# Hybrid decoder step on one core: the last down weight's low parts move from GpSimd to VectorE, and the closing tiles move forward

## The reference, cut to what matters

```python
h = h + jnp.concatenate([y_conv, y_ret], axis=-1) @ w_out
hn2 = rmsnorm(h, norm_mlp)
h = h + jnp.square(jax.nn.relu(hn2 @ w_up)) @ w_down      # w_down: 4096 x 1024, f32
y_prompt = rmsnorm(hp, norm_final)[:, N_META:]
y_sample = rmsnorm(hs, norm_final)
```

## Time and profile before

| | |
|---|---|
| median of 3 runs | 1129.34 us (1129.16 to 1129.98) |
| profiled execution | 1129.29 us, span 1127.4 us, mean granted TensorE clock 0.998 |
| PE busy | 1116.3 us, 99% of the span |
| DVE, POOL, ACT busy | 785.9, 560.2, 418.8 us |
| HBM traffic | 133 GB/s over the span |

### The profile page before, as it was taken

How to read it: one execution, slowest core, us unless ns; L and a number is a source line. 1 busy time by engine, 2 the same in 40 slices (tenths; PEclk the granted TensorE clock), 3 DMA queues, 4 the chain that set the end, 5 groups by cost and what they waited for, 6 DMA issues and landing times.

```text
span 1127.4 us, 21934 instructions
## 1 busy us (share of the span) xinstructions
PE 1116.3 (99%) x8351; PEld 1097.5 (97%) x8351; DVE 785.9 (70%) x1170; ACT 418.8 (37%) x864; POOL 560.2 (50%) x542
## 2 busy tenths in 40 slices
PE   9999999999999999999999999999999999999997
PEld 7799999999999999999999999999999999999996
DVE  5555656566466766888776777767877777877856
ACT  6422313123124343543333333335552544444424
POOL 0054253252240601142322323224999899999995
PEclk9999999999999999999999999999999999999999
DMA  8951341422323232155344353438962444464314
GB/s 221 236 138 52 97 120 49 130 75 77 94 77 96 77 113 76 60 186 188 114 151 151 133 177 114 151 114 299 328 192 75 153 151 149 134 189 151 94 38 151
DMA packets 188347, 151.41 MB, mean 134 GB/s; under 512 B 33086, under 2 KB 150566, under 8 KB 188256
## 3 DMA queue, kind: packets, MB, share of 16 engines
q1 hardware_dynamic: 183159, 146.98, 41.6%
q10 hardware_dynamic: 5096, 3.20, 0.9%
HBM read 105.44 MB, written 44.73 MB: 133 GB/s over the span
## 4 chain that ended last, share of the span: by engine, by line
PE 97%; issue 1%; DMA 1%; SPq 0%; POOL 0%; POOLq 0%; DVE 0%
PE pair L2127 19%; PE pair L2128 19%; PE pair L2129 19%; PE pair L1921 8%; PE pair L1923 8%; PE pair L1922 8%; PE pair L2106 3%; PE pair L2105 3%; PE pair L2104 3%; PE pair L1979 1%; PE pair L1980 1%; PE pair L1982 1%; PE pair L2029 1%; PE pair L2032 1%; PE pair L2039 1%
## 5 line engine op out<-in xcount | busy, mean ns | idle before, releaser
L2127 PE MATMUL pair<-m_hi,dn_hi 128*128 128x258 f32 (+2 forms) x896 | 254.7, 284 | 0.6 <-issue 0.5
L2128 PE MATMUL pair<-b_lo,up_hi 128*128 128x258 f32 x896 | 253.6, 283 | 0.0
L2127 PE MATMUL pair<-b_hi,up_hi 128*128 128x258 f32 x896 | 253.6, 283 | 0.0
L2128 PE MATMUL pair<-m_lo,dn_hi 128*128 128x258 f32 (+2 forms) x896 | 253.6, 283 | 0.0
L2129 PE MATMUL pair<-m_hi,dn_lo 128*128 128x258 f32 (+2 forms) x896 | 253.4, 283 | 0.0
L2129 PE MATMUL pair<-b_hi,up_lo 128*128 128x258 f32 x896 | 252.2, 282 | 0.0
L1921 PE MATMUL pair<-x_hi,w_both 128*128 128x344 f32 (+2 forms) x576 | 188.6, 328 | 0.1
L1923 PE MATMUL pair<-x_hi,w_both 128*128 128x344 f32 (+2 forms) x576 | 184.5, 320 | 0.0
L1922 PE MATMUL pair<-x_lo,w_both 128*128 128x344 f32 (+2 forms) x576 | 184.2, 320 | 0.0
L1888 DVE TENSOR_TENSOR hid<-pair,hid 128x516 f32<-128x516 f32 (+2 forms) x194 | 124.6, 643 | 73.8 <-PE pair L2129 71.0
L2127 PEld LDWEIGHTS pair<-b_hi,up_hi 128*128 128x128 f32 x896 | 169.3, 189 | 1.0 <-issue 0.8
(11 more groups left out here) (232 smaller groups left out, 2052.7 us busy)
## 6 DMA issues: line engine op xcount, KB each, us to landing
m_raw<-m_dram SPq DMA_DIRECT2D x56, 516.0 KB, 4.9
m_dram<-hid SPq DMA_DIRECT2D x64, 258.0 KB, 3.7
up_raw<-w_up_dram SPq DMA_DIRECT2D x32, 512.0 KB, 4.9
dn_raw<-w_down_dram SPq DMA_DIRECT2D x128, 128.0 KB, 2.4
w_raw<-w_in_dram SPq DMA_DIRECT2D x27, 512.0 KB, 3.7
m_dram<-hid SPq DMA_DIRECT2D x16, 774.0 KB, 3.8
h_dram<-hid SPq DMA_DIRECT2D x8, 516.0 KB, 3.1
h_in<-h_dram SPq DMA_DIRECT2D x16, 258.0 KB, 6.1
```

The source lines that it names most:

```text
L2127: m_.matmul(to, shs[k], mhs[k], start=STARTS[i] and k == 0, stop=False, skip_group_check=more)
L2128: m_.matmul(to, shs[k], mls[k], start=False, stop=False, skip_group_check=more)
```

## The change

- GpSimd makes no low parts of the last weight (`wi` = 31). VectorE makes them (`last_low`), one each after the reads named in `LOW_AT`, in units 29 and 30. GpSimd goes from the last `down_sum` to its closing work, and closes unit 31 read by read, as it does units 32 to 34.
- The transposes of tiles 0 to 4 and their scalings are placed earlier (`FINAL_AT`, `NORM_AT`): from the second product of unit 32 to the last of unit 33.
- VectorE adds three of the late squares into `sq_sum` after its last read, so that `token_sums` is one product for each tile where it was three or two. ScalarE does all four `last_square` before `late_std`, and the squares of unit 33 (`piece_squares(2)`) after tile 4.
- The store of tile 6 is cut from 120 rows into 112 and 8.
- At the start ScalarE writes the first head's high part before the small transfers of the row norms; at the end of the up projection it writes the last two high parts of the first down weight before two hidden splits.

```diff
-FINAL_AT = {(NW, 6): 0, (NW + 1, 1): 1, (NW + 1, 4): 2, (NW + 1, 6): 3, (NW + 2, 2): 4}
-NORM_AT = {(NW + 1, 1): (0, 0), (NW + 1, 2): (0, 1), (NW + 1, 3): (1, 0), (NW + 1, 4): (1, 1), (NW + 1, 6): (2, 0), (NW + 2, 0): (2, 1),
-           (NW + 2, 2): (3, 0), (NW + 2, 3): (3, 1), (NW + 2, 5): (4, None)}
+FINAL_AT = {(NW, 1): 0, (NW, 3): 1, (NW + 1, 0): 2, (NW + 1, 3): 3, (NW + 1, 6): 4}
+NORM_AT = {(NW, 4): (0, 0), (NW, 5): (0, 1), (NW, 6): (1, 0), (NW + 1, 0): (1, 1), (NW + 1, 3): (2, 0), (NW + 1, 4): (2, 1),
+           (NW + 1, 6): (3, 0), (NW + 2, 0): (3, 1), (NW + 2, 2): (4, None)}
+LOW_AT = {(HALVES, 0): 0, (HALVES, 2): 1, (HALVES, 4): 2, (HALVES, 6): 3, (HALVES + 1, 1): 4, (HALVES + 1, 3): 5, (HALVES + 1, 5): 6}
...
-                    sp.dma_start(io["y_prompt"][0, r0:r0 + n - more, :], y[0:n - more, :]).then_inc(y_stored[i % 4], 16)
+                    full = n - 2 * more
+                    sp.dma_start(io["y_prompt"][0, r0:r0 + full, :], y[0:full, :]).then_inc(y_stored[i % 4], 16)
                     if more:
+                        sp.dma_start(io["y_prompt"][0, r0 + full:r0 + n - more, :], y[full:n - more, :]).then_inc(y_stored[i % 4], 16)
...
             for wi in range(NW):
                 down_sum(wi)
-                for i in range(7):
-                    down_low(wi, i)
+                if wi < NW - 1:
+                    for i in range(7):
+                        down_low(wi, i)
...
-                    pool.wait_ge(dn_read, 7 * q + (seen if q >= NW else 7))
+                    pool.wait_ge(dn_read, 7 * q + (seen if q >= NW - 1 else 7))
...
+            act.wait_ge(w_gained, 1)
+            high(0, 0, None)
             act.wait_ge(rstdx_done, XT)
...
-            act.wait_ge(w_gained, 1)
-            high(0, 0, None)
             act.wait_ge(rx_moved, 48)
...
+                        if i == 5:
+                            down_split(0, 5)
+                            down_split(0, 6)
                         for j in ((), (0,), (1,), (2,), (3,), (4, 5), ())[i]:
                             mid_split(j)
-                        down_split(0, i)
+                        if i < 5:
+                            down_split(0, i)
...
-                if i == REST:
-                    piece_squares(2)
...
-            for i in range(3):
+            piece_squares(2)
+            for i in range(4):
                 last_square(i)
             late_std(0)
-            last_square(3)
             late_std(1)
...
+            def last_low(i):
+                n = dn_slot(NW - 1)
+                dve.wait_ge(dn_ready, 7 * (NW - 1))
+                dve.wait_ge(dn_high, 7 * (NW - 1) + i + 1)
+                d.tensor_tensor(dn_lo[n][i][:, :, :], dn_source(NW - 1, i), dn_hi[n][i][:, :, :], ALU.subtract).then_inc(dn_ready, 1)
...
-                        if q >= NW and i >= 5:
+                        if q >= NW - 1 and i >= 5:
                             dve.wait_ge(closed, 3 * (q - NW + 4) + i - 4)
...
+                    if (q, p) in LOW_AT:
+                        last_low(LOW_AT[(q, p)])
...
+            for i in range(1, 4):
+                which = LAST_ORDER[i]
+                total = sq_sum[:, which % 2, :]
+                dve.wait_ge(hsq_done, GROUPS + 7 + i)
+                dve.wait_ge(ssq_done, GROUPS - 2 + 6)
+                if i > 1:
+                    dve.wait_ge(late_added, i - 1)
+                d.tensor_tensor(total, total, sq_last[:, which, :], ALU.add).then_inc(late_added, 1)
...
-                pe.wait_ge(ssq_done, GROUPS - 2 + (6 if LATE_L[j] == 0 else 5))
-                pe.wait_ge(hsq_done, GROUPS + GROUP_AT[j])
+                pe.wait_ge(late_added, LATE_ADDED[j])
+                if j:
+                    pe.wait_ge(fstd_done, FIRST_LATE + 1)
...
-                    src = [sq_sum[:, LATE_L[j], c0:c1]] + [sq_last[:, which, c0:c1] for which in GROUP[j]]
-                    for k, sq in enumerate(src):
-                        ins = m_.matmul(SUM_B[:, 2 * j + tile:2 * j + tile + 1], sq, ones[:, 0:1], start=k == 0, stop=k == len(src) - 1)
+                    ins = m_.matmul(SUM_B[:, 2 * j + tile:2 * j + tile + 1], sq_sum[:, LATE_L[j], c0:c1], ones[:, 0:1], start=True, stop=True)
...
+                if i == 0:
+                    pe.wait_ge(dn_read, 7 * NW)
```

More of the change, by code:

```diff
@@ L150 @@
 LAST_ORDER, LAST_READ = (0, 3, 1, 2), (4, 5, 6, 7)
-GROUP, GROUP_AT = ((3, 1), (2,)), (9, 10)
+LATE_ADDED = (2, 3)
 LW = EDGE[2] - EDGE[1]
@@ L357, in late_rows, with dn_source @@
             return [(acc(n, first + a)[:, EDGE[1]:EDGE[2]].unsqueeze(1), slice(a, a + 1)) for a in range(2)]
+        def dn_source(wi, i):
+            return dn_raw[wi % 2][:, 2 * A_OP[i][0] + A_OP[i][1], :, :] if i in (0, 2, 5) else dn_s[A_OP[i]][:, :, :]
         def acc(n, which):
@@ L404, in program @@
         o_done, o_read, Sinc_done, S_ready = sem("o_done"), sem("o_read"), sem("Sinc_done"), sem("S_ready")
-        std_ready, o_normed, yT_done, y_ready = sem("std_ready"), sem("o_normed"), sem("yT_done"), sem("y_ready")
+        std_ready, o_normed, y_ready = sem("std_ready"), sem("o_normed"), sem("y_ready")
         ksmp_ready, state_dec, state_new = sem("ksmp_ready"), sem("state_dec"), sem("state_new")
@@ L430, in program @@
             "fT_done", "fsq_done", "fstd_done", "frstd_done", "f_ready"))
-        d_half = sem("d_half")
+        d_half, late_added = sem("d_half"), sem("late_added")
         dve_own, passed = sem("dve_own"), sem("passed")
@@ L747, in _ @@
                     more = SAMPLES if l and c1 == HALF else 0
-                    sp.dma_start(io["y_prompt"][0, r0:r0 + n - more, :], y[0:n - more, :]).then_inc(y_stored[i % 4], 16)
+                    full = n - 2 * more
+                    sp.dma_start(io["y_prompt"][0, r0:r0 + full, :], y[0:full, :]).then_inc(y_stored[i % 4], 16)
                     if more:
+                        sp.dma_start(io["y_prompt"][0, r0 + full:r0 + n - more, :], y[full:n - more, :]).then_inc(y_stored[i % 4], 16)
                         sp.dma_start(io["y_sample"].rearrange("b s d -> (b s) d"), y[n - more:n, :]).then_inc(y_stored[i % 4], 16)
-            for i, count in enumerate((5, 3, 3, 2)):
+            for i, count in enumerate((5, 3, 4, 2)):
                 sp.wait_ge(y_stored[i], 16 * count)
@@ L882, in down_low @@
                 n = dn_slot(wi)
-                src = dn_raw[wi % 2][:, 2 * A_OP[i][0] + A_OP[i][1], :, :] if i in (0, 2, 5) else dn_s[A_OP[i]][:, :, :]
+                src = dn_source(wi, i)
                 pool.wait_ge(dn_high, 7 * wi + i + 1)
@@ L1287, in piece_squares @@
                 act.wait_ge(closed, 3 if n == 0 else 12 + 3 * n)
+                if n == 0:
+                    act.wait_ge(dn_ready, 7 * NW)
                 act.wait_ge(dn_read, 7 * (NW - 3 if n == 0 else NW + n))
```

## The result

| kernel | median us (runs) | ratio to before, 95% interval |
|---|---|---|
| before | 1129.4 (8) | |
| after | 1132.3 (8) | 1.0025, 1.0016 to 1.0034 |

The change makes the kernel 2.8 us slower (1.8 to 3.8 us by the interval). The profiled execution of after took 1131.3 us, 1.0 under its own median; its span is 1129.5, 2.1 over that of before. So the pair of traces shows 2.0 of the 2.8 us; the other 0.8 is in no trace. VectorE's reads now stand at line 1907, its low parts at 1848, its late adds at 1930; GpSimd's closing adds at 909; TensorE's products at 2156 to 2158, its transposes at 2228, the token sums at 2200.

A forecast was written before the change was run, and what follows sets the result against it. TensorE, busy for 99% of the span, was taken to bound the kernel. The terms −0.2 − 0.3 + 0.8 + 1.3 + 0.4 + 0.5 + 0 = +2.5 on 1129.29 gave 1131.8 us, range 1128.4 to 1133.4.

The forecast's parts named there:

- Start: At the kernel's start, ScalarE's high part moved ahead lets TensorE begin earlier: −0.2 us, bounds 0 to −0.4.
- First down weight: First down unit: earlier high parts shift GpSimd's phase against VectorE's hidden low part: −0.3 us, bounds −0.6 and +0.2.
- Inputs: Unit 29: VectorE's low part 1 waits for ScalarE's high part, delaying the fifth read and TensorE's seventh product: +0.8 us.
- Collision: Units 29 and 30: VectorE's low parts wait through whole GpSimd closing adds: +1.3 us, bounds 0 and +1.9.
- Closing tiles: Unit 33: uncovered wait before the seventh product, tile 2's transposes before tile 0 is scaled: +0.4 us, bounds 0 and +0.6.
- Tail: After the last product: late `add_last` and VectorE adds delay token sums, dropped passes give some back: +0.5 us.
- Stores: Store of tile 6 at the end: extra issue is covered, bytes are the same: 0 us.
- only the high part's wait counts: Rival: VectorE and GpSimd collide little, so the collision term and half the tiles' go: 1130.3 us, chance 0.25.
- the change is not slower: Rival: GpSimd reaches the last weight's sums earlier, second sum done by 1080.7, low parts cost nothing: 1128.4 us, chance 0.15.
- growing lag: Rival: low part 0 delays GpSimd's sums, low parts 2 to 5 each meet a full long add: 1133.4 us, chance 0.10.

The follow-up runs named there:

- tiles alone: Kernel before with only the closing tiles' places and the square order that belongs to them changed: 1135.34 us, ratio 1.0052.
- sums alone: Kernel before with only the late squares added by VectorE and the token sums in one pass: 1129.12 us, ratio 0.9997.
- low parts later: Kernel before with low parts on VectorE behind later reads, GpSimd's closing adds held until all are written, unit 31 closed read by read: 1132.49 us.
- free: Kernel before with late low parts on VectorE and held closing adds, unit 31 closed as before: 1129.38 us, ratio 0.9999.
- sums split: Kernel before with the first token sums' passes over sq_sum issued ahead of the wait for the last squares: 1128.6 us, ratio 0.9994.
- low parts held: Kernel before with low parts on VectorE, unit 31 closed read by read, GpSimd's closing adds waiting until all low parts are written: 1135.61 us.
- old store: The changed kernel with the 120-row store of tile 6 again: 1132.24 us, ratio 1.0026.
- transposes first: The changed kernel with the transposes of tile 5's rest and of tile 6 ahead of the token sums: 1131.73 us, ratio 1.0021.
- low parts alone: Kernel before with only the low parts moved to VectorE and GpSimd closing unit 31 read by read: 1131.67 us, ratio 1.0018.
- Split sums with the store: Kernel before with split token sums, the 112-row store and the first high part moved ahead: 1128.03 us, ratio 0.9987.

## Why the prediction was right, point by point

The prediction was 1131.8 us, the median is 1132.3. The profiled pair differs by 2.0 us where the sum gave 2.5. That the number lies so near the median is in part luck: the tail's +0.5 did not come, and the medians differ by 0.8 more than the pair, for which no trace has a place. What held is the mechanism of the two largest terms, inputs and collision, which the experiments isolate.

- **Start**, −0.2: from the eight matmuls to the first head product it is 1.84 us where the earlier trace rows have 2.10, −0.26. Right, and 1.84 too in the two kernels that have this edit without the low parts and tiles. Timeline of after:

```profile
54.12 1.06 ACT L952 ACTIVATE w_both<-w_raw 128x1024 fp32r<-128x1024 f32 x1 [1.63 <-POOL w_raw L774]
...
58.02 2.00 PE L1986 MATMUL pair<-wv_lo,x_end 128*24 128x512 f32 x8
...
59.86 0.33 PE L1950 MATMUL pair<-x_hi,w_both 128*128 128x360 f32 x1
```

- **First down weight**, −0.3: not shown. In after TensorE waits 0.37 and 0.30 us there in place of 0.54, and unit 29 comes 0.42 earlier in all. But with the same edits alone the waits summed to 1.9 us and the time did not move. How VectorE and GpSimd meet differs between executions by more than this term: among six kernels with the same code up to there (before, tiles alone, sums alone, low parts later and free, sums split), unit 29's seventh product starts between 1081.68 and 1083.49.
- **Inputs**, +0.8: 1.05. The mechanism is right: low parts held apart from GpSimd leave this loss whole, later places remove it. The size is 0.25 low, mostly because low part 0 holds GpSimd up: its first sum took 0.91 us beside it, 0.17 more than the 0.74 of a sum that meets no low part, and the second sum, on which the high part waits, moves by as much. I had this in the upper bound only.
- **Collision**, +1.3: 0.27 + 0.74 = 1.01. Shown by the held kernel: low part 2 takes 0.42 in place of 1.54 and unit 30's losses go. One by one, GpSimd's adds end at 1084.34, 1085.79, 1087.22 and 1088.82, and low parts 2 to 5, each begun inside one of them, end 0.28 to 0.29 us behind these: VectorE stood through the whole instruction each time, as the prediction had it. The size is 0.3 high because unit 29 had already lost 0.25 more; the two terms together are 2.06 where the sum had 2.1. That their sum fits so well is luck in part: GpSimd's adds began 0.37 us later against unit 29 than assumed, and a low part ended 0.28 behind an add, not the 0.55 of the earlier trace rows. The Trainium skill's exclusive lock (SBUF — State Buffer, "SBUF: two separate sides") agrees with this trace: 1.54 us for a low part that began 0.04 us into a closing add of 1.29. The Trainium skill's other rule (GPSIMD Engine Reference, "Engine selection") is about right on the price, 0.42 against GpSimd's 0.74. That price is worth nothing here, since GpSimd's low parts were not what TensorE waited for.
- **Closing tiles**, +0.4: from unit 31's seventh product to E 21.65 us (1094.76 to 1116.41) against 21.11 (1093.03 to 1114.14), +0.54. Two more traces of the changed kernel, with the old store and with the transposes first, have 21.64 and 21.62; low parts alone has 21.11. Of the 0.54, 0.34 stand at tile 2's transposes, which wait for VectorE's scaling as predicted:

```profile
1103.46 1.06 PE L2228 MATMUL pair<-ident,hid 128*128 128x128 f32 x8 [0.18 <-DVE y_out L1838]
```

- **Tail**, +0.5: −0.17. The steps up to the first scaling are right: `add_last` at E + 1.31 (predicted 1.35), first token sums E + 2.45 (2.2), first scaling +0.89 (+0.6). The difference is that VectorE's adds start 0.56 apart, not 0.4, and that the first waits for a square of ScalarE's too, done 0.07 behind `add_last`. The step that failed is the last one, from VectorE's scalings and ScalarE's half tile to the end: the last issue came 1.75 later instead of 0.2 to 0.3, and the end did not move. Half of the 1.75 is a clock of 0.50 in the transposes, which kernels with before's own tail show as well, so that half is not the change's. The sum took it that the end follows VectorE and ScalarE; the table of the tails shows slack there, and an end of −0.17 is well within its spread.
- **Stores**, 0: no difference in time with the old store.

Of the rivals, that only the high part's wait counts falls with the 1.01 us of collision; that the change is not slower falls with GpSimd's second sum, done at 1081.45 where 1080.7 was needed. The growing lag did not come: low part 0 did delay the sums, but by 0.17 us, and low parts 3 to 6 took 0.41 to 1.00 us.

What the prediction did not see: closing unit 31 read by read adds a wait of VectorE for GpSimd, and only GpSimd's lead in the changed order keeps it free.

## What to carry to other kernels

Before work moves from an idle-looking engine to the one that feeds the bottleneck, look at what stands behind it in that engine's order and when its inputs are ready: the same seven instructions cost 2.0 us in the changed places, and nothing where their inputs were there, GpSimd was held still and unit 31 was closed as before. Parts of a schedule change are not additive, so test each alone and price the waits that one part keeps free for another. At the end of a kernel, measure from the last issue to the end first; where stores fill that time, an engine finishing later or earlier may not show. And look at several traces of the same code before reading a difference of a microsecond out of two.

## What the runs showed of the hardware

- TensorE that stood 2.56 us (tiles alone) and 3.52 us (low parts held) was granted a mean of 0.60 and 0.59 over the 3.7 us that followed, most of it at 0.50 (1.2 GHz); after 2.14 us in the kernel with later low parts it kept 1.00. The length of the stop alone does not tell: in after TensorE stood 2.45 us behind the last product, and the windows from 1119 to 1121 still have 1.00.
- In the tail the granted clock fell to 0.50 (1.2 GHz) in every trace, but at different places: behind the transposes in before and with split sums (20 transposes in 2.52 us), within them elsewhere (up to 4.51 us). Split sums with the store has the same TensorE code there and took 4.51.
- The collision goes both ways: GpSimd's sums of 0.74 us took 0.91 and 0.98 beside VectorE's low parts of 0.42, and its adds of 516 columns, at most 1.33 in before, took 1.50 and 1.47.
